# Decode attention keys turned in 32x32 blocks on VectorE instead of 128x128 on TensorE

## The chip, the core and the metric

The kernel runs on one core of a Trainium2 chip. The metric is the device time of one execution in microseconds; lower is better. In the profile PE is TensorE (matmuls), PEld its weight loads, DVE VectorE, ACT ScalarE, POOL GpSimd and SP the engine that issues most DMAs. SBUF has 128 partitions; a PSUM bank holds 128 partitions of 512 fp32 numbers.

## What is computed

One step of a two-layer decoder for a prompt of 512 tokens and a sample group of 8 sequences with 8 new tokens each, which have 2048 past tokens in a paged cache. Layer 0 is differential attention, layer 1 retention. The change touches only the sample group's attention over the cache:

```python
kp = cache_k[page_table].reshape(db, past, nh, 2, d)      # pages of 128 tokens, 8 heads, k1 | k2, d = 128
vp = cache_v[page_table].reshape(db, past, nh, -1)        # 256 wide
s_past = jnp.einsum('bqhcd,bkhcd->bchqk', q, kp)
s_new = jnp.einsum('bqhcd,bkhcd->bchqk', q, k_new)
sc = jnp.concatenate([s_past, s_new], axis=-1) * scale - slopes[:, None, None] * dist[None]
p = jax.nn.softmax(jnp.where(dist >= 0, sc, -jnp.inf), axis=-1)
p = p[:, 0] - lam * p[:, 1]
return einsum('bhqk,bkhe->bqhe', p[..., :past], vp) + einsum('bhqk,bkhe->bqhe', p[..., past:], v_new)
```

A score needs the 128 numbers of a head's key on the partitions, and a page arrives with its tokens on the partitions, so every page has to be turned. All is fp32.

## The kernel before

**Projections.** The bulk of the kernel is the projection matmuls (PE `project`, helper `mm`, L965). A weight chunk of 4x128x256 is split by ACT (WH, L1236) and DVE (WL, L1523) into a high and a low part, and each 128x128 weight tile meets the activations as WH·XH, WH·XL and WL·XH, each as two matmuls of 288 columns: six matmuls are one "projection tile". The program is written as one list of stages; `proj.tile()` is the beat, and everything else stands at a numbered slot before a tile (`attention_pair`, 256 slots for a pair of heads; `page_slot(k)` = 2 + 3.5 k). Every engine runs its own part of each stage in the list's order and waits on semaphores.

**The sample group's attention** is worked off in eight halves of 128 slots (a pair of heads, four of the eight sequences). In a half:

- `carry` (DVE, L1681), just ahead of the half, copies the new queries and keys (at the middle of a pair, "qk") or the new values and gates (at its end, "vg") out of the projection's results. `place_q` (DVE, L1599) at slot 0 spreads the queries into `qrow`, with zeros, so that the four sequences of a half fall on different rows.
- `load_k` (SP, L903) fetches a page of 128 tokens x 512 numbers (256 KB) into one of 4 ring places `Kr`. `page` turns it: 4 TensorE transposes of 128x128 (PE L1032, helper `tr`, L968) into bank 4 for even and bank 5 for odd pages; ACT copies the even ones to `KTs` (L1357, copy helper L1236), DVE the odd ones (L1605, the copy is L1610). Two pages stand at one slot, and such a pair comes every 3.5 slots: 64 pages in a half, 512 in all.
- A unit is four pages of one sequence. `qk` (PE L1040) multiplies it: four matmuls of 512 columns, each into its own 32 rows of bank 6 (two heads x two key halves). There are 16 units in a half, one every 7 slots. After four units (one from each sequence, added up in the bank) `row_scores` (DVE L1613) adds the bias and takes a maximum.
- `soft_new`, `soft_max`, `soft_exp`, `soft_norm` stand at slots 28, 118, 120 and 125. `soft_new` (PE L1050) is four matmuls of 64 columns into 32 rows each.
- In the next half `e_transpose` (slots 7, 11) turns the probabilities, and `value` (PE L1069) multiplies four pages of values by them, every 7 slots from slot 16 on, at the slot of a `qk`. `load_v` (SP L909) fetches four pages into a ring of 8 behind each `value`. Each value page has its own semaphore. `sample_sq` (slot 127 of every second half) needs DVE's `soft_norm` and mixing to be done.

SP is one queue: between slot A and slot A + 7 it issues four value loads, two key loads, two more key loads and most times one weight load (L890), in this order. A page's number is read from `pt` ahead of each cache load (L900).

Of the kernel before, what the change touches and what calls it, by code (L numbers as in the profile page):

```python
# [17 lines left out]
HEADS = 8  # L18
# [13 lines left out]
NPAIR = 1 + NGROUP + 1  # L32
# [3 lines left out]
def shape_tables():  # L36
# [7 lines left out]
    head, half, tok, own_b = r // 64, r // 32 % 2, r % 32 // BATCH, r % BATCH  # L44
    dist_past = PAST + tok[:, None] - np.arange(GROUP * PAGE)[None]
    out_head, out_tok = r % 32 // 16, r % NQ
    pick = (out_head[:, None] == np.arange(2)[None]).repeat(NQ, 1) * np.tile(out_tok[:, None] == np.arange(NQ)[None], (1, 2))
    rows = np.concatenate([dist_past, pick, (half == 0)[:, None], (half == 1)[:, None]], 1)
    row = np.arange(SMP)
    pairs = []  # L50
    for g in range(HEADS // 2):
        sl = slope[2 * g + head][:, None]
        ahead = sl * GROUP * PAGE * np.arange(NGROUP)[None]
        dn = tok[:, None] - (row % NQ)[None]
        new = [np.where((row[None] // NQ == (BATCH * q + own_b)[:, None]) & (dn >= 0), -sl * dn, MASKED) for q in range(2)]
        pairs.append(np.concatenate([-sl, ahead, 0 * sl] + new, 1))
# [34 lines left out]
def adds(s):  # L91
# [26 lines left out]
    if k == "store_x":  # L118
# [18 lines left out]
        "place_q": {"q_placed": 1},  # L137
# [31 lines left out]
    if k == "load_v":  # L169
        return {f"v_in{a['n'] % VRING}": 16}  # L170
    if k in ("page", "e_transpose"):
        n = 4 + a["n"] % 2
        return {f"full{n}": 1, f"drained{n}": 1}
# [77 lines left out]
class SampleAttention:  # L251

    def __init__(self):
        self.pages = [(a, q, kg, bl, kg * GROUP + pp) for a in range(HEADS // 2) for q in range(2) for kg in range(NGROUP)
                      for bl in range(BATCH) for pp in range(GROUP)]
# [4 lines left out]
    def load_k(self):  # L260
        n = self.k_loads
        if n >= len(self.pages):
            return []
        self.k_loads += 1
        a, q, _, bl, p = self.pages[n]
        return [Stage("load_k", n=n, pair=a, b=BATCH * q + bl, p=p, freed=self.page_of.get(n - KRING))]
# [9 lines left out]
    def keys(self, h):  # L276
# [5 lines left out]
        put(0, Stage("place_q", pair=h // 2, q=h % 2))  # L282
        units = NGROUP * BATCH
        for u in range(units):
            kg, bl = divmod(u, BATCH)
            for pp in range(GROUP):
# [3 lines left out]
                if pp == 0 and u:  # L290
                    put(slot(u * GROUP + pp), *self.scores(h, u - 1))
                put(slot(u * GROUP + pp), page, *self.load_k())
        put(page_slot(2 * units), *self.scores(h, units - 1))
# [6 lines left out]
    def scores(self, h, u):  # L300
        kg, bl = divmod(u, BATCH)
        n = (h * NGROUP * BATCH + u) * GROUP
        qk = Stage("qk", u=u, bl=bl, last_even=self.page_of[n + 2], last_odd=self.page_of[n + 3])
        self.qk_of[h * NGROUP * BATCH + u] = qk
        return [qk] + ([Stage("row_scores", kg=kg)] if bl == BATCH - 1 else [])
# [374 lines left out]
def hybrid_step_kernel(nc, x_prompt, x_sample, cache_k, cache_v, page_table, state_ret, norm_pre_attn, w_in_attn,  # L680
# [30 lines left out]
    with ctx:  # L711
# [34 lines left out]
        qT0, kT0, vT, vn0, kn = lay("qT0", [128, 2, T]), lay("kT0", [128, 2, T]), lay("vT", [128, 2, T]), lay("vn0", [128, 5, 256]), lay("kn", [128, 2, 256])  # L746
# [5 lines left out]
        sgS, vS = [lay(f"sgS{i}", [128, 4, SMP]) for i in range(2)], [lay(f"vS{i}", [128, 512]) for i in range(2)]  # L752
        sS, sN = lay("sS", [128, PAST]), lay("sN", [128, SMP])
        e_all, e_new = lay("e_all", [128, PAGES, 128]), lay("e_new", [SMP, 128])
        dist_past, picks = lay("dist_past", [128, GROUP * PAGE]), lay("picks", [128, 18])
        pair_row = lay("pair_row", [128, NPAIR + 2 * SMP])
        KTs = [lay(f"KTs{i}", [128, 4, GROUP * PAGE]) for i in range(2)]
        qrow = lay("qrow", [128, 4, 132])
        row_sign, oV = lay("row_sign", [128, 1]), lay("oV", [128, 512])
        gmax, ebias, lsum, row1 = lay("gmax", [128, 5]), lay("ebias", [128, 5]), lay("lsum", [128, 5]), lay("row1", [128, 2])  # L760
        oS, oQ = lay("oS", [128, 4, SMP]), lay("oQ", [128, 4, SMP])
        rsS = lay("rsS", [128, 128])
        sc, pT = lay("sc", [128, 2, 512]), lay("pT", [128, 512])
# [24 lines left out]
        used[0] = 6 * T  # L788
# [88 lines left out]
        def _(sp):  # L877
# [21 lines left out]
            def load_page(src, pair, b, p, to):  # L899
                page = sp.value_load(pt[0:1, b * PAGES + p:b * PAGES + p + 1], min_val=0, max_val=src.shape[0] - 1)  # L900
# [1065 lines left out]
```

## Time and profile before

| | us |
|---|---|
| median of 3 runs (3840.97 to 3844.4) | 3841.65 |
| span of the profiled execution, first to last instruction | 3828.5 |
| the difference, around the span | 13.15 |
| attention, first to last key load | 135 to 1635 |
| PE busy | 3709.1 (97%) |
| DVE busy | 1453.5 (38%) |
| ACT busy | 1123.9 (29%) |

PE's busy time is a union of matmuls that overlap; what an edit on PE is worth is read from the starts of the instructions in the timeline, not from durations. A matmul of fp32 with 32 weight columns appears as two records, a transpose as one, a projection matmul as one.

### The profile page before, as it was taken

To read this page: it belongs to the slowest core of one execution; us is meant where nothing else is said; L and a number is where in the kernel's file an instruction comes from. 1 tells how busy PE (TensorE), PEld (TensorE's weight loads), DVE (VectorE), ACT (ScalarE), POOL (GpSimd) and SP (SyncE) were. 2 spreads that over 40 slices of the span, in tenths; PEclk is the share of its full clock that TensorE was granted. 3 is DMA by queue.
4 is the path that set the end of the run, shared out by engine and by line. 5 is a ranking of instruction groups with operands and counts; after the bars stand their busy time and mean duration, and the time that the engine had idled before them with its cause. 6 is when DMAs were issued, how large, how long until landed. Compare 5 with 4: busy or idle time off the path is not lost.

```text
span 3828.5 us, 70107 instructions
## 1 busy us (share of the span) xinstructions
PE 3709.1 (97%) x26980; PEld 3275.7 (86%) x26980; DVE 1453.5 (38%) x2215; ACT 1123.9 (29%) x1808; POOL 150.6 (4%) x87
## 2 busy tenths in 40 slices
PE   7999999999999999989899999999999999999998
PEld 7987887888788877767898989999989899989998
DVE  4244334433443344323633333333333324243345
ACT  4233233323332333221422222222222222232223
POOL 1000000200020002002200000000000000000000
PEclk9999999999999999999999999999999999999999
DMA  5456778687768776764442525242424343443333
GB/s 172 151 177 188 239 239 237 212 244 236 238 210 245 238 237 215 244 197 168 135 139 83 165 83 166 79 164 85 160 86 161 94 149 98 163 138 130 108 122 121
DMA packets 472204, 642.91 MB, mean 168 GB/s; under 512 B 35649, under 2 KB 294850, under 8 KB 468738
## 3 DMA queue, kind: packets, MB, share of 16 engines
q1 hardware_dynamic: 407122, 565.92, 47.6%
q10 hardware_dynamic: 64336, 72.24, 5.6%
q8 instruction: 216, 3.54, 0.4%
q14 instruction: 114, 0.93, 0.1%
q0 software_dynamic: 416, 0.28, 0.1%
HBM read 566.09 MB, written 70.65 MB: 166 GB/s over the span
## 4 chain that ended last, share of the span: by engine, by line
PE 50%; DVE 2%; issue 1%; DMA 1%; ACT 1%; POOL 1%; SPq 1%; ACTq 0%; DVEq 0%; POOLq 0%
PE low_banks L965 42%; PE high_banks L965 6%; PE high_banks L968 1%; DMA area<-in_cache_v 1%; POOL area L1897 1%; DVE WL L1523 0%; ACT WH L1236 0%; DMA WR<-in_w_in_ret 0%; SPq L900 0%; SPq L901 0%; ACTq L1401 0%; DVE area L1782 0%; ACT area L1236 0%; DVE area L1545 0%; ACTq L1400 0%
## 5 line engine op out<-in xcount | busy, mean ns | idle before, releaser
L965 PE MATMUL low_banks<-XH,WH 128*128 128x288 f32 (+2 forms) x6656 | 1545.6, 310 | 42.0 <-DVE XL L1528 16.6
L965 PE MATMUL low_banks<-XH,WL 128*128 128x288 f32 (+2 forms) x6656 | 1455.4, 296 | 0.0
L965 PE MATMUL low_banks<-XL,WH 128*128 128x288 f32 (+2 forms) x6656 | 1452.6, 296 | 0.0
L965 PEld LDWEIGHTS low_banks<-XH,WH 128*128 128x128 f32 x6656 | 1080.4, 190 | 142.4 <-issue 96.0
L965 PEld LDWEIGHTS low_banks<-XH,WL 128*128 128x128 f32 x6656 | 1083.7, 189 | 0.0
L965 PEld LDWEIGHTS low_banks<-XL,WH 128*128 128x128 f32 x6656 | 1083.4, 189 | 0.0
L1523 DVE TENSOR_TENSOR WL<-WR,WH 128x1024 fp32r<-128x1024 f32 x436 | 533.4, 1223 | 817.8 <-ACT WH L1236 812.7
L1236 ACT ACTIVATE WH<-WR 128x1024 fp32r<-128x1024 f32 x436 | 461.2, 1058 | 923.4 <-PE low_banks L965 652.6
L965 PE MATMUL high_banks<-area 128*32 128x512 f32 (+8 forms) x3696 | 654.1, 547 | 16.1 <-DVE area L1554 5.6
L1236 ACT ACTIVATE area<-high_banks 128x512 f32<-128x512 f32 x480 | 270.2, 569 | 1139.4 <-PE high_banks L968 756.8
L968 PEld LDWEIGHTS high_banks<-eye_sb,area 128*128 128x128 f32 (+2 forms) x3080 | 352.4, 142 | 156.6 <-issue 116.8
L968 PE MATMUL high_banks<-eye_sb,area 128*128 128x128 f32 (+2 forms) x3080 | 439.1, 278 | 40.9 <-DVE area L1857 15.8
L965 PEld LDWEIGHTS high_banks<-area 128*32 128x32 f32 (+4 forms) x3696 | 239.6, 147 | 231.5 <-issue 205.0
L1610 DVE COPY area<-high_banks 128x512 f32<-128x512 f32 x256 | 177.0, 691 | 569.8 <-PE high_banks L968 477.7
L1897 POOL TENSOR_TENSOR area<-area,power 128x1 f32<-128x1 f32 (+4 forms) x67 | 126.6, 1890 | 3639.6 <-DVE area L1495 3168.9
L1299 ACT ACTIVATE area<-low_banks 128x288 f32<-128x288 f32 (+2 forms) x384 | 157.9, 411 | 346.8 <-PE low_banks L965 311.6
L1545 DVE TENSOR_TENSOR area<-low_banks,area 128x288 f32<-128x288 f32 (+2 forms) x160 | 73.2, 457 | 144.4 <-PE low_banks L965 134.7
L1782 DVE SCALAR_TENSOR_TENSOR area<-area,high_banks 128x512 f32<-128x512 f32 x128 | 87.2, 744 | 49.8 <-PE high_banks L965 49.8
L1763 DVE SCALAR_TENSOR_TENSOR area<-area,high_banks 128x512 f32<-128x512 f32 x48 | 35.8, 747 | 159.9 <-PE high_banks L965 157.9
L1795 DVE TENSOR_TENSOR area<-high_banks,area 128x512 f32<-128x512 f32 (+1 forms) x40 | 25.6, 640 | 113.5 <-PE high_banks L968 113.5
L1618 DVE SCALAR_TENSOR_TENSOR area<-area,high_banks 128x512 f32<-128x512 f32 x32 | 23.9, 747 | 66.6 <-PE high_banks L965 66.6
L1528 DVE TENSOR_TENSOR XL<-XL,XH 128x576 fp32r<-128x576 f32 (+1 forms) x48 | 36.1, 752 | 31.9 <-ACT XH L1236 30.7
(113 smaller groups left out, 840.9 us busy)
## 6 DMA issues: line engine op xcount, KB each, us to landing
area<-in_cache_k SPq DMA_DIRECT2D x512, 256.0 KB, 4.1
area<-in_cache_v SPq DMA_DIRECT2D x512, 256.0 KB, 4.1
WR<-in_w_in_ret SPq DMA_DIRECT2D x200, 512.0 KB, 3.5
WR<-in_w_in_attn SPq DMA_DIRECT2D x136, 512.0 KB, 5.4
out<-area ACTq DMA_DIRECT2D x73, 512.0 KB, 3.1
WR<-in_w_out_ret SPq DMA_DIRECT2D x68, 512.0 KB, 3.3
area<-in_state_ret SPq DMA_DIRECT2D x64, 512.0 KB, 5.6
WR<-in_w_out_attn SPq DMA_DIRECT2D x32, 512.0 KB, 5.5
```

Source lines behind the costliest of these rows:

```text
L965: return nc.tensor.matmul(out, a, b, start=start, stop=stop, skip_group_check=True)
L968: return nc.tensor.matmul(out, a, ident[0:n, 0:n], start=True, stop=True, is_transpose=True, skip_group_check=True)
L1236: return nc.scalar.activation(out, in_, ACT.Copy, scale=scale)
L1299: last = nc.scalar.activation(dst[:, lo:hi], bank[2 * cb + b][:, 0:hi - lo], f)
L1523: v.tensor_tensor(WL[:, slot, :, :], WR[:, slot, :, :], WH[:, slot, :, :].bitcast(f32), SUB).then_inc(sem["w_lo"], 1)
L1528: v.tensor_tensor(XL[:, kt, 0:width], XL[:, kt, 0:width].bitcast(f32), XH[:, kt, 0:width].bitcast(f32), SUB).then_inc(sem["w_lo"], 1)
L1545: last = v.tensor_tensor(dst[:, lo:hi], bank[2 * cb + b][:, 0:hi - lo], dst[:, lo:hi], ADD)
L1610: v.tensor_copy(KTs[u % 2][:, :, pp * 128:(pp + 1) * 128], bank[5][:, :].rearrange("p (j s) -> p j s", j=4)).then_inc(sem["drained5"], 1)
L1763: ins = v.scalar_tensor_tensor(out=Sp[:, e, :], in0=Sp[:, e, :], scalar=hc[:, 387:388], in1=bank[4 + e][:, :], op0=MUL, op1=ADD)
L1782: v.scalar_tensor_tensor(out=mine, in0=mine, scalar=hc[:, 388:389], in1=bank[4 + j][:, :], op0=MUL, op1=ADD).then_inc(sem[f"drained{4 + j} ...
L1795: v.tensor_tensor(to, o4, g4, MUL).then_inc(sem[f"drained{n}"], 1)
L1897: nc.gpsimd.tensor_tensor(out, a, power[0:R, 0:n], ALU.pow).then_inc(sem[name], 1)
```

## The change

Keys are turned by DVE in SBUF, in blocks of 32x32, and PE no longer touches the pages before `qk`. One DVE instruction takes two pages (128 x 2 x 16 x 32) into the new layout `KTs` [128, 16, 128]: block m holds the 32 numbers 32 m .. 32 m + 31 of the keys, on partition 32 a + i stands number i of token quarter a. The stages stay at their slots; `page` does nothing for the first page of a pair, and both key loads stand behind the second. The order of units changes: all four units of one sequence come one after the other, so `row_scores` is by sequence.

`qk` becomes 16 matmuls of 128 columns for a unit (four blocks of the head's 128 numbers, added up, for each of four 32-row outputs) with queries that are zero except in the rows of their token quarter. `place_q` makes these queries with 16 PE matmuls against slices of the identity and four DVE copies. PE's first act in a half is now to wait for `carried`. Softmax statistics are shared among the four quarters of a token by small DVE transposes (`stat`, `row_all`). Value pages are loaded so that their tokens follow the new order: 32 partitions at a stride of 4, four places each; the four pages of a group raise one semaphore.

```diff
         "place_q": {"q_placed": 1},
+        "place_q": {"full4": 1, "drained4": 1},
...
-                put(slot(u * GROUP + pp), page, *self.load_k())
+                put(slot(u * GROUP + pp), page, *([*self.load_k(), *self.load_k()] if pp % 2 else []))
...
             def load_k(g, n, pair, b, p, freed):
                 if freed is not None:
-                    bank_sem = f"full{4 + freed.a['n'] % 2}"
-                    sp.wait_ge(sem[bank_sem], c.after(freed, bank_sem))
+                    sp.wait_ge(sem["k_turned"], c.after(freed, "k_turned"))
...
+                sp.dma_start(Vr[t:128:GROUP, half * GROUP:(half + 1) * GROUP, :],
+                             cv[page, :, pair * 512:(pair + 1) * 512].rearrange("a (o j) n -> j (a o) n", o=4)
+                             ).then_inc(sem[f"v_in{half}"], 16)
...
-            def page(g, n, u, pp, freed):                       # PE
-                ...
-                for j in range(4):
-                    last = tr(bank[b][:, j * 128:(j + 1) * 128], Kr[:, slot, j * 128:(j + 1) * 128])
+            def place_q(g, pair, q):                            # PE
+                pe.wait_ge(sem["carried"], c.before("carried"))
+                free(4)
+                ...
+                for d in range(4):
+                    for a in range(4):
+                        last = mm(spread[32 * a:32 * a + 32, d], ident[:, 32 * d:32 * d + 32], mine)
+                last.then_inc(sem["full4"], 1)
...
+            def qk(g, u, bl, kg, placed, turned):
+                pe.wait_ge(sem["k_turned"], c.after(turned, "k_turned"))
+                pe.wait_ge(sem["drained4"], c.after(placed, "drained4"))
                 pe.wait_ge(sem["s_drained"], c.before("s_drained"))
-                for j in range(4):
-                    last = mm(bank[6][32 * j:32 * j + 32, :], qrow[:, j, 32 * bl:32 * bl + 32], KTs[u % 2][:, j, :],
-                              start=bl == 0, stop=bl == BATCH - 1)
+                for d in range(4):
+                    for j in range(4):
+                        last = mm(bank[6][32 * j:32 * j + 32, kg * 128:(kg + 1) * 128], qrow[:, bl * 16 + 4 * j + d, :],
+                                  KTs[u % 2][:, 4 * j + d, :], start=d == 0, stop=d == 3)
...
             def page(g, n, u, pp, freed):                       # DVE
+                if pp % 2 == 0:
+                    return
+                slot = n % KRING - 1
+                for k in (slot, slot + 1):
+                    dve.wait_ge(sem[f"k_in{k}"], START[f"k_in{k}"] + 16 * (n // KRING + 1))
+                if freed is not None:
+                    dve.wait_ge(sem["qk_done"], c.after(freed, "qk_done"))
+                v.transpose(KTs[u % 2][:, :, 32 * pp - 32:32 * pp + 32].rearrange("p m (t i) -> p t m i", t=2),
+                            Kr[:, slot:slot + 2, :].rearrange("p t (m i) -> p t m i", i=32)).then_inc(sem["k_turned"], 1)
```

On DVE `row_scores` becomes four additions of 128 columns and a maximum in place of one addition of 512 and a maximum; `soft_max` goes from 3 to 5 instructions; `soft_norm` from 5 (the last over 2048 columns) to 12 (the last four over 512 each). ACT loses its copies of the even pages.

On PE, at a unit with values in the second half (before): the value matmuls, `qk` (32x512) and the transposes of two pages stand between two projection tiles.

```order
L965 MATMUL high_banks<-area 32x512 [waits pv_drained,v_in0,drained5,drained4]
L965 MATMUL high_banks<-area 32x512 [waits v_in1]
L965 MATMUL high_banks<-area 32x512 [waits v_in2]
L965 MATMUL high_banks<-area 32x512 [waits v_in3]
L965 MATMUL high_banks<-area 32x512 [waits q_placed,s_drained,drained5,drained4]
L965 MATMUL high_banks<-area 32x512 x3
L968 MATMUL high_banks<-eye_sb,area 128x128 [waits drained4,k_in0]
L968 MATMUL high_banks<-eye_sb,area 128x128 x3
L968 MATMUL high_banks<-eye_sb,area 128x128 [waits drained5,k_in1]
L968 MATMUL high_banks<-eye_sb,area 128x128 x3
L965 MATMUL low_banks<-XH,WH 128x288 [waits w_lo]
```

The same place on PE now:

```order
L975 MATMUL high_banks<-area 32x512 [waits pv_drained,v_in0,drained5,drained4]
L975 MATMUL high_banks<-area 32x512 x3
L975 MATMUL high_banks<-area 32x128 [waits s_drained,drained4,k_turned]
L975 MATMUL high_banks<-area 32x128 x15
L975 MATMUL low_banks<-XH,WH 128x288 [waits w_lo]
```

The transposes and PE's waits for key loads are gone, and `qk` waits for DVE's `k_turned`.

On PE, at the start of a half (before); the projection goes on at once:

```order
L965 MATMUL low_banks<-XH,WH 128x288 [waits proj0_drained,x_lo,w_lo]
L965 MATMUL low_banks<-XH,WH 128x288
L965 MATMUL low_banks<-XL,WH 128x288 x2
L965 MATMUL low_banks<-XH,WL 128x288 x2
```

The same place on PE now; `32x16x8` are the matmuls of `place_q`:

```order
L975 MATMUL low_banks<-XL,WH 128x288 x2
L975 MATMUL low_banks<-XH,WL 128x288 x2
L975 MATMUL high_banks<-area,eye_sb 32x16x8 [waits drained4,carried]
L975 MATMUL high_banks<-area,eye_sb 32x16x8 x15
L975 MATMUL low_banks<-XH,WH 128x288 [waits proj0_drained,x_lo,w_lo]
L975 MATMUL low_banks<-XH,WH 128x288
```

All projection tiles of the half now stand behind a wait for `carried`.

On DVE, in a half with prompt work (before): a copy of an odd page, then the parts of the output and of a weight chunk.

```order
L1610 COPY area<-high_banks 128x4x128 [waits qk_done,full5]
L1592 SCALAR_TENSOR_TENSOR area<-high_banks,subln,area 128x128 [waits proj1_drained,gated_out,proj0_drained,full4]
L1592 SCALAR_TENSOR_TENSOR area<-high_banks,subln,area 128x128 [waits dve_order]
L1610 COPY area<-high_banks 128x4x128 [waits qk_done,full5]
L1523 TENSOR_TENSOR WL<-WR,WH 128x1024 [waits w_hi]
```

The same place on DVE now:

```order
L1623 STREAM_TRANSPOSE area<-area 128x2x16x32 [waits qk_done,k_in1,k_in0]
L1597 SCALAR_TENSOR_TENSOR area<-high_banks,subln,area 128x128 [waits proj1_drained,gated_out,proj0_drained,full4]
L1597 SCALAR_TENSOR_TENSOR area<-high_banks,subln,area 128x128 [waits dve_order]
L1623 STREAM_TRANSPOSE area<-area 128x2x16x32 [waits qk_done,k_in3,k_in2]
L1528 TENSOR_TENSOR WL<-WR,WH 128x1024 [waits w_hi]
```

The wait for the key loads (`k_in`) has moved from PE to DVE, ahead of the work queued there.

## Rows read from the trace of the kernel before

**Rows 1.** The page, part 1: busy us, share of the span, instructions.

```profile
PE 3709.1 (97%) x26980; PEld 3275.7 (86%) x26980; DVE 1453.5 (38%) x2215; ACT 1123.9 (29%) x1808; POOL 150.6 (4%) x87
```

**Rows 2.** Windows over seven runs of 14 blocks: window, length, busy, clock, DMA, GB/s.

```profile
527.50:680.60 153.10, 151.16 (x1147) 122.02 (x1146) 57.50 (x106) 49.06 (x87) 2.56 (x3) 1.00 0.82 246
...
sum 1069.90, PE 1051.74 PEld 846.07 DVE 403.69 ACT 324.88 POOL 16.45; mean PE 150.25 PEld 120.87 DVE 57.67 ACT 46.41 POOL 2.35
```

**Rows 3.** Timeline of PE over one unit: start, length, instruction, count, idle before.

```profile
207.47 0.43 PE L965 MATMUL low_banks<-XH,WL 128*128 128x288 f32 x2
207.83 1.06 PE L965 MATMUL high_banks<-area 128*32 128x512 f32 x8
208.83 1.09 PE L968 MATMUL high_banks<-eye_sb,area 128*128 128x128 f32 x8
209.68 0.51 PE L965 MATMUL low_banks<-XH,WH 128*128 128x288 f32 x2
...
212.15 1.03 PE L968 MATMUL high_banks<-eye_sb,area 128*128 128x128 f32 x8
212.94 0.52 PE L965 MATMUL low_banks<-XH,WH 128*128 128x288 f32 x2
213.29 0.43 PE L965 MATMUL low_banks<-XL,WH 128*128 128x288 f32 x2
```

**Rows 4.** Timeline of PE at `soft_new`: short matmuls of 32 weight columns.

```profile
178.36 0.32 PE L965 MATMUL high_banks<-area 128*32 128x64 f32 x8
178.61 0.53 PE L965 MATMUL low_banks<-XH,WH 128*128 128x288 f32 x2
178.98 0.29 PE L965 MATMUL low_banks<-XL,WH 128*128 128x288 f32 x1
```

**Rows 5.** Lines by form: busy, mean ns of one, idle before and releaser.

```profile
L1523 DVE TENSOR_TENSOR WL<-WR,WH 128x1024 fp32r<-128x1024 f32 x436 | 533.4, 1223 | 817.8 <-ACT WH L1236 812.7 <-issue 3.8
L965 PE MATMUL high_banks<-area 128*32 128x512 f32 x2304 | 306.8, 608 | 5.1 <-DMA area<-in_cache_v 3.2 <-DVE area L1652 1.7
L1610 DVE COPY area<-high_banks 128x512 f32<-128x512 f32 x256 | 177.0, 691 | 569.8 <-PE high_banks L968 477.7 <-issue 89.7 <-DVE WL L1523 1.1
L1775 DVE TENSOR_SCALAR area<-area 128x512 f32<-128x512 f32 x40 | 18.0, 485 | 5.6 <-POOL area L1897 5.3
L965 PE MATMUL high_banks<-area 128*32 128x64 f32 x64 | 2.6, 231 | 0.0
```

**Rows 6.** Timeline of DVE and then PE around the middle of a pair ("qk").

```profile
502.38 1.29 DVE L1642 TENSOR_SCALAR area<-area 128x2048 f32<-128x2048 f32 x1
...
508.67 0.23 DVE L1694 COPY area<-area 128x128 f32<-128x128 f32 x1
...
506.18 0.43 PE L965 MATMUL low_banks<-XH,WH 128*128 128x288 f32 x2
```

**Rows 7.** Timeline of DVE and then PE around the end of a pair ("vg").

```profile
699.81 0.29 DVE L1687 COPY area<-area 128x256 f32<-128x256 f32 x1
...
697.67 0.42 PE L965 MATMUL low_banks<-XH,WH 128*128 128x288 f32 x2
```

**Rows 8.** Timeline of SP's DMA issues over one block (start, from first to last issue).

```profile
548.94 3.64 SPq L901 DMA_DIRECT2D area<-in_cache_v  x4
553.38 3.66 SPq L901 DMA_DIRECT2D area<-in_cache_k  x4
557.09 0.96 SPq L890 DMA_DIRECT2D WR<-in_w_in_attn  x1
```

**Rows 9.** The key loads by tile: issue ns min/median/max; us to landing min/median/max.

```profile
L901 SPq DMA_DIRECT2D area<-in_cache_k x512: 332/333/976, 135.3 to 1634.8; - x171
...
DMA to landing us min/median/max: 2.9/4.1/8.5
```

**Rows 10.** Waits of SP's queue from 330 to 1640: total us, times, longest.

```profile
SPq L900 <- PE high_banks L965: 141.9, 85, 4.5
SPq L900 <- PE high_banks L968: 87.3, 65, 11.9
```

More of the change, by code:

```diff
@@ L52, in shape_tables @@
         sl = slope[2 * g + head][:, None]
-        ahead = sl * GROUP * PAGE * np.arange(NGROUP)[None]
         dn = tok[:, None] - (row % NQ)[None]
-        new = [np.where((row[None] // NQ == (BATCH * q + own_b)[:, None]) & (dn >= 0), -sl * dn, MASKED) for q in range(2)]
-        pairs.append(np.concatenate([-sl, ahead, 0 * sl] + new, 1))
+        new = [np.where((row[None] // NQ == (BATCH * q + quarter)[:, None]) & (dn >= 0), -sl * dn, MASKED) for q in range(2)]
+        pairs.append(np.concatenate([-sl] + new, 1))
     bias_pairs = np.stack(pairs)
@@ L169, in adds @@
     if k == "load_v":
[L170 to L171 removed]
+        return {f"v_in{a['n'] // GROUP % 2}": 16}
+    if k == "page":
+        return {"k_turned": 1} if a["pp"] % 2 else {}
+    if k == "e_transpose":
         n = 4 + a["n"] % 2
@@ L281, in keys @@
         slot = lambda n: page_slot(n // 2)
-        put(0, Stage("place_q", pair=h // 2, q=h % 2))
+        placed = Stage("place_q", pair=h // 2, q=h % 2)
+        put(0, placed)
         units = NGROUP * BATCH
         for u in range(units):
-            kg, bl = divmod(u, BATCH)
             for pp in range(GROUP):
@@ new lines, in row_scores @@
+            def row_scores(g, bl):
+                cols = slice(bl * 512, (bl + 1) * 512)
+                for n in ("qk_done", "full4", "full5", "bias_sample_in"):
+                    dve.wait_ge(sem[n], c.before(n))
+                in_turn = lambda a: a.rearrange("p (j t) -> p j t", t=GROUP)
+                for kg in range(NGROUP):
+                    part = slice(kg * 128, kg * 128 + 128)
+                    ins = v.scalar_tensor_tensor(out=in_turn(sS[:, bl * 512 + kg * 128:bl * 512 + kg * 128 + 128]), in0=in_turn(dist_past[:, part]),
+                                                 scalar=pair_row[:, 0:1], in1=bank[6][:, part].rearrange("p (t j) -> p j t", t=GROUP),
+                                                 op0=MUL, op1=ADD)
+                    if kg < NGROUP - 1:
+                        o.link(ins)
+                    else:
+                        ins.then_inc(sem["s_drained"], 1)
@@ new lines, in soft_norm @@
+                o.link(v.transpose(stat_T[:], stat[:]))
+                o.link(v.reduce_sum(stat_8[:], by_token, AX.X))
+                o.link(v.reciprocal(stat_8[:], stat_8[:]))
+                rows_back()
+                o.link(v.tensor_scalar(row_all[:, 0:BATCH], row_all[:, 0:BATCH], row_sign[:], None, MUL))
+                o.link(own_row(row_new[:]))
+                o.link(v.tensor_scalar(sN[:], sN[:], row_new[:], None, MUL))
+                for n in range(BATCH):
+                    part = sS[:, n * 512:(n + 1) * 512]
+                    ins = v.tensor_scalar(part, part, row_all[:, n:n + 1], None, MUL)
+                    if n < BATCH - 1:
+                        o.link(ins)
+                    else:
+                        ins.then_inc(sem["e_normed"], 1)
```

157 lines of the change are left out of this document (74 added, 83 removed).

## The prediction, made before the changed kernel had been run

> **What bounds the kernel now.** The page's first part says PE: 97% busy, DVE 38%, ACT 29% [rows 1]. That average hides stages, so I read the windows over the seven runs of 14 blocks in which keys and values are both loaded (a block is 7 slots, from one `qk` to the next): PE is busy 1051.7 of 1069.9 us, DVE 404, at full clock [rows 2]. A block lasts 1069.9 / 98 = 10.92 us on average. So an instruction taken from PE there is time won, unless the next limit comes first. The next limit is not DVE but SP's queue. In the SP timeline four cache loads take 3.64 us from the first to the last issue, of which the last issue is 0.33, so one load occupies the queue for (3.64 - 0.33) / 3 = 1.10 us [rows 8, 9]. A block needs eight of them, 8.8 us, and most times a weight load, 0.4 to 1.0 [rows 8]: 9.5 us. In the wait view SP was held by PE for 141.9 + 87.3 = 229 us between 330 and 1640 [rows 10]: that is its reserve, and the change eats into it.
>
> **Edit 1: pages off PE, `qk` in short matmuls.** From the PE timeline over one unit without values [rows 3]. Before: `qk` starts 0.36 us after the last projection step's start where a step takes 0.26 (entry 0.10); `qk` and the first two pages take from 207.83 to 209.68 (1.85); the second two pages 0.79 (212.15 to 212.94), and the step after them 0.35 where 0.26 is usual (0.09), which holds after the first two pages as well. Sum 0.10 + 1.85 + 0.09 + 0.88 = 2.92 us a unit.
> After: 16 matmuls of 128 columns, four side by side in four groups of 32 weight columns, each two records: eight rounds. How long is a round? At 512 columns two rounds take 1.06 - 0.61 = 0.45 for the distance of one [rows 3, 5]. At 64 columns the distance is 0.32 - 0.23 = 0.09 [rows 4, 5]. The line through both gives 0.14 for 128; without any fixed part, 0.45 / 4 = 0.11. I take 0.125, since in a series the next weights can load under the running round. Entry 0.10 as above; exit by `soft_new`: 0.25 to the next projection step less two rounds of 0.09, and 0.37 for that step instead of 0.26, together 0.18 [rows 4]. Sum 0.28 + 8 x 0.125 = 1.28 us. A unit saves 1.64 (1.52 to 1.78). There are 8 x 16 = 128: **-210 us** (-195 to -228). 512 ACT and DVE copies go too, from engines with room: nothing.
>
> The trace's short matmuls give 0.02 to 0.03 us of fixed part in a round. The Trainium skill, page "TensorEngine Tiling (Array Packing)", section "Performance Considerations", has each matmul carry some 60 cycles. An estimate from that page, if all 32 records of a unit paid it in turn, is 0.8 us a unit, and the gain would shrink by about 100 us.
>
> **Edit 2: `place_q` on PE, behind `carried`.** 16 matmuls of 128 columns like `qk`: 8 x 1.28 = **+10 us**. Before them PE waits for DVE's `carry`, and all projection tiles of the half are queued behind that wait. At a "qk" boundary PE began slot 128 at 506.18 and `carry` ended at 508.67 + 0.23 = 508.90: 2.7 us [rows 6]. At a "vg" boundary 697.67 and 700.10: 2.4 [rows 7]. Four of each: **+20 us**. It can't be hidden: `carry` needs the last tile's evacuation, which PE has only just fed. Then DVE makes four copies of 512 columns from PSUM, 4 x 0.69 [rows 5], before bank 4 is free; PE's prompt `scores` at slot 2 want it. And `soft_norm` ends in four instructions of 512 columns (0.485 each, [rows 5]) instead of one of 1.29 [rows 6], plus seven small ones: about 1.7 us later for `sample_sq` at slot 127, four times. Against that, short waits of PE that were there shrink. Together **+6 us** (0 to 20).
>
> **Edit 3: DVE turns.** 256 instructions of 2 x 512 numbers. No row shows one. Nearest: the weight split, 1024 numbers a partition from SBUF to SBUF, 1.22 us [rows 5]; I take that. A floor is one copy of 512, 0.69; a ceiling twice 1.22, should a turn pass numbers at half that rate. At 1.22 DVE gains 2 x (1.22 - 0.69) = 1.1 us a block on 404 / 98 = 4.1 [rows 2, 5], 5.2 in 9.3: it has room. But it now waits for the keys, ahead of its weight splits and the prompt's softmax. After slot A the queue issues four values, then two keys; the second is issued at about A + 1 + 4.4 + 1.9 = 7.3 us and lands 4.1 later [rows 9], at A + 11.4, while DVE's place in the program comes at A + 9.3. So DVE stands some 2 us in every block. PE asks for the block's turned keys only 3.5 slots later and for a weight split 6 tiles later; I put **+8 us** (0 to 30) for the prompt's chain.
>
> **The queue.** A block on PE becomes 10.92 - 1.64 = 9.28 us, SP needs 9.5. On average that is 0.22 x 98 = 22 us, if SP could run ahead without limit. It can't: key places are four, so long blocks give nothing back. Against that stands a lag of about 3 us that PE tolerates in each of the seven runs. I take 3 us a run: **+21 us** (0 if the lag absorbs it, 45 if a value load in the new form [32, 4] takes 0.1 us longer to issue, which is 0.4 x 98 = 39 more less the tolerance). In the tail, where PE only waits for values, all four loads must be in: **+2 us**.
>
> **Sum.** -210 + 10 + 20 + 6 + 8 + 21 + 2 = -143. The sum is made on the profiled execution: 3828.5 - 143 = 3685.5, with the 13.15 around the span 3698.6 against the median. I say 3698.
>
> **Rivals.**
> - *Neither queue nor keys hold anyone.* SP has 229 us of waits in reserve [rows 10]. Then -210 + 38 = -172: 3670. Against it: 9.28 is below 9.5.
> - *DVE becomes the bound.* At 2.45 us a turn, DVE has 4.1 - 1.4 + 4.9 = 7.6 us of work and 2 of waiting in a block, 9.6, in order, and stalls of PE on top: some 0.5 us x 98 = 49 on top, 3747. For it: no row shows a turn. The Trainium skill, page "VectorE: DVE Perf Modes", section "The three transpose paths", gives 311 ns for a 128x128 turn on VectorE in bf16. An estimate from that page, eight times as much for two pages, is 2.5 us; the trace's rows have no turn to set beside it.
> - *Short rounds cost 0.20 us*, because four weight loads a round don't hide under 128 columns: 8 x 0.075 x 136 = +82, 3780. `soft_new`'s 0.09 at 64 columns speaks against it [rows 4, 5].
> - *Slower than before: the value loads.* Each now writes four places on 32 partitions at a stride. If such a load holds SP longer by x, a block is 9.5 + 4x. Outside the 98 blocks the change gains 30 x 1.64 - 38 = 11 us, 0.11 a block, so it decides from 9.5 + 4x = 11.03, x = 0.38 us, i.e. 1.48 a load instead of 1.10. At x = 0.5: 98 x (11.5 - 11.03) = +46, 3888. Issues of 0.33 have few outliers (up to 0.98, [rows 9]).
>
> **How the numbers follow.** Forecast 3698 (its own range 3665 to 3730): 0.58. First rival 0.15, DVE 0.12, rounds 0.08, value loads 0.05; 0.02 for about no change. The range must hold 0.8: 3650 (rounds of 0.11 and a free queue: -228 + 38 = -190) to 3760 (the DVE rival and part of the queue's bound); the last three cases lie outside. A measurement of this kernel can tell 0.2% from no change. Faster by more than that 0.92, within it 0.02, slower 0.06.
>
> **What would show it.** PE records of 128 columns on 32 weight columns, 2048 matmuls for `qk`, a unit of 1.28 us between projection steps, no transposes of pages. A DVE turn of about 1.2 us, 256 times, with waits on key loads. At each half's start a PE wait of 2 to 3 us on DVE's `carry`. SP waits far below 229 us and blocks with values at 9.4 to 9.6. It would be wrong if those blocks reached 10 us, if a turn took over 2 us, or if the value loads landed later than 4 us.

## The result, and the profile after

The changed kernel takes 3853.6 us (median of 11 runs, 3842.8 to 3863.5), the kernel before 3837.8 (11 runs, 3827.8 to 3844.4). The ratio is 1.0039, 95% interval 1.0028 to 1.0049: slower by 0.4%. The forecast was 3698, the range 3650 to 3760, and it gave "slower" 0.06.

The page of the changed kernel, part 1, against [rows 1]:

```profile
span 3851.8 us, 71863 instructions
PE 3566.1 (93%) x28260; PEld 3196.8 (83%) x28260; DVE 1647.2 (43%) x2424; ACT 983.2 (26%) x1552; POOL 150.7 (4%) x87
```

PE's busy time fell by more than 140 us and the span rose by 23.3. That compares two single executions; by the medians the change costs 15.8. (The 13.15 us that I had called "around the span" are mostly this scatter: the timed executions on record are only 1.8 to 2.8 us longer than their spans, so the profiled one of before was a quick one. The forecast, 143 us under the median, does not depend on it.) What was won as work came back as waiting. Where, the wait view from 130 to 1640 tells (us in total, times, longest):

```profile
DVE area L1623 <- DMA area<-in_cache_k: 521.3, 185, 12.4
...
PEld high_banks L975 <- DVE area L1623: 98.7, 49, 8.4
...
PE high_banks L975 <- DVE area L1623: 63.0, 34, 8.2
```

PE and its weight loads wait for turned keys (L1623), and DVE, which turns them, stands 521 us for the key loads. The loads themselves, by line (issue in ns, min/median/max; us from issue to landing), first the keys, to be set beside [rows 9], then the values:

```profile
L913 SPq DMA_DIRECT2D area<-in_cache_k x512: 327/333/1162, 132.8 to 1633.4; - x171
...
DMA to landing us min/median/max: 2.9/4.3/8.7
```

```profile
L920 SPq DMA_DIRECT2D area<-in_cache_v x512: 602/602/1192, 266.4 to 1770.3; - x171
...
DMA to landing us min/median/max: 3.6/4.3/7.4
```

Both land as fast as keys did before, to 0.2 us. But a value load in its new shape holds SP 0.60 us instead of 0.33. The SP timeline over one block, answering [rows 8] (start, from first to last issue, instruction, count):

```profile
549.16 4.92 SPq L920 DMA_DIRECT2D area<-in_cache_v  x4
554.87 3.68 SPq L913 DMA_DIRECT2D area<-in_cache_k  x4
558.59 0.43 SPq L897 DMA_DIRECT2D WR<-in_w_in_attn  x1
559.80 4.74 SPq L920 DMA_DIRECT2D area<-in_cache_v  x4
```

From one value group to the next 10.64 us pass, and what lies between the issues is register work: with 4.75 for four value issues one load takes (4.75 - 0.60) / 3 = 1.38 us, before 1.10. In the wait view of SP from 514 to 650 there are 4.3 us of waits in 136; SP's long waits (175.8 us for L1623 between 130 and 1640) lie elsewhere: 72 us before 320, where only keys are loaded, and most of the rest at the half boundaries. Inside the halves with values **the queue sets the pace**. A block of 10.6 us is also past the 10 at which the prediction called itself wrong.

### The profile page after: what moved, and what is told of

It is laid out like the page before. It is cut to its first block, busy times and chain, and to the rows that moved or that the text cites. A ratio compares the mean times of both kernels' runs of the same rounds, so it can differ in the third digit from the quotient of the medians.

```text
span 3851.8 us, 71863 instructions
## 1 busy us (share of the span) xinstructions
PE 3566.1 (93%) x28260; PEld 3196.8 (83%) x28260; DVE 1647.2 (43%) x2424; ACT 983.2 (26%) x1552; POOL 150.7 (4%) x87
## 4 chain that ended last, share of the span: by engine, by line
PE 50%; DVE 1%; issue 1%; SPq 1%; ACT 1%; POOL 1%; DMA 1%; ACTq 0%; DVEq 0%; POOLq 0%
PE low_banks L975 43%; PE high_banks L975 6%; PE high_banks L978 1%; POOL area L1939 1%; DMA area<-in_cache_v 1%; SPq L920 0%; DVE WL L1528 0%; SPq L907 0%; ACT WH L1248 0%; ACTq L1405 0%; DVE area L1824 0%; ACT area L1248 0%; ACT XH L1248 0%; DVE area L1550 0%; DMA WR<-in_w_in_ret 0%
## 5 line engine op out<-in xcount | busy, mean ns | idle before, releaser
L975 PEld LDWEIGHTS low_banks<-XH,WH 128*128 128x128 f32 x6656 | 1097.5, 192 | 189.5 <-issue 125.6
L975 PE MATMUL high_banks<-area 128*32 128x128 f32 (+6 forms) x6768 | 677.8, 392 | 127.4 <-DVE area L1623 63.0
L975 PEld LDWEIGHTS high_banks<-area 128*32 128x32 f32 (+2 forms) x6768 | 331.4, 135 | 351.8 <-issue 218.5
L1623 DVE STREAM_TRANSPOSE area<-area 128x1024 f32<-128x1024 f32 x256 | 318.7, 1245 | 548.1 <-DMA area<-in_cache_k 521.3
L1248 ACT ACTIVATE area<-high_banks 128x512 f32<-128x512 f32 (+1 forms) x224 | 119.1, 537 | 646.0 <-PE high_banks L978 341.9
L978 PE MATMUL high_banks<-eye_sb,area 128*128 128x128 f32 (+2 forms) x1032 | 160.8, 278 | 51.3 <-DVE area L1899 16.0
L978 PEld LDWEIGHTS high_banks<-eye_sb,area 128*128 128x128 f32 (+2 forms) x1032 | 124.1, 142 | 57.1 <-issue 47.4
L1824 DVE SCALAR_TENSOR_TENSOR area<-area,high_banks 128x512 f32<-128x512 f32 x128 | 87.2, 745 | 50.1 <-PE high_banks L975 50.1
L1805 DVE SCALAR_TENSOR_TENSOR area<-area,high_banks 128x512 f32<-128x512 f32 x48 | 35.8, 747 | 159.8 <-PE high_banks L975 157.9
L1322 ACT ACTIVATE area<-area 128x128 f32<-128x128 f32 (+3 forms) x64 | 36.0, 563 | 115.8 <-DVE area L1563 100.1
L1633 DVE SCALAR_TENSOR_TENSOR area<-area,high_banks 128x128 f32<-128x128 f32 x128 | 44.5, 347 | 23.9 <-PE high_banks L975 14.6
```

The source lines that it names most:

```text
L975: return nc.tensor.matmul(out, a, b, start=start, stop=stop, skip_group_check=True)
L978: return nc.tensor.matmul(out, a, ident[0:n, 0:n], start=True, stop=True, is_transpose=True, skip_group_check=True)
L1248: return nc.scalar.activation(out, in_, ACT.Copy, scale=scale)
L1322: ins = nc.scalar.activation(sc[:, cc, 0:n], sc[:, cc, 0:n], ACT.Exp, bias=pst[:, cc:cc + 1], accum_out=pst[:, 2 + cc:3 + cc])
L1623: v.transpose(KTs[u % 2][:, :, 32 * pp - 32:32 * pp + 32].rearrange("p m (t i) -> p t m i", t=2), Kr[:, slot:slot + 2, :].rearrange("p t ( ...
L1633: ins = v.scalar_tensor_tensor(out=in_turn(sS[:, bl * 512 + kg * 128:bl * 512 + kg * 128 + 128]), in0=in_turn(dist_past[:, part]), scalar= ...
```

## One stretch in nine kernels

From the second unit of the second half to its last value group lie 15 unit intervals, the same work in each kernel. I read its length with the windows view. Columns: window, length, then busy time of PE, PEld, DVE, ACT, POOL (instructions), granted clock, DMA share, GB/s. Before, then changed:

```profile
527.46:688.30 160.84, 158.90 (x1205) 128.14 (x1205) 61.46 (x115) 50.88 (x92) 3.11 (x4) 1.00 0.81 243
```

```profile
513.00:672.20 159.20, 142.67 (x1341) 118.84 (x1340) 78.43 (x130) 34.02 (x60) 3.10 (x4) 0.95 0.83 245
```

PE has 16 us less to do and the stretch is 1.6 us shorter. The experiments below fill this table (the lengths are read in the same way from one profiled run each; medians of whole runs beside them; e1's profiled run is 15 us under its median, e2's 9 over):

| kernel | stretch, us | per unit | clock | whole, us |
|---|---|---|---|---|
| before | 160.8 | 10.72 | 1.00 | 3838 |
| before, strided values (e2) | 169.0 | 11.27 | 1.00 | 3895 |
| before, no bounds test (e9) | 160.6 | 10.71 | 1.00 | 3820 |
| before, fixed pages (e10) | 160.3 | 10.69 | 1.00 | 3807 |
| changed | 159.2 | 10.61 | 0.95 | 3854 |
| changed, plain values (e1) | 148.9 | 9.93 | 0.97 | 3762 |
| changed, no bounds test (e5) | 143.5 | 9.57 | 1.00 | 3712 |
| changed, fixed pages (e6) | 137.0 | 9.13 | 1.00 | 3657 |
| changed, fixed pages, plain values (e11) | 136.9 | 9.13 | 1.00 | 3657 |

## Experiments: the queue and the order of loads

Theory Q says that SP's work per block sets the pace. Its rivals: B, pauses of PE at the boundaries; K, keys issued behind values; S, the strided shape as such.

**e1, changed kernel with plain value loads.**

```diff
-                sp.dma_start(Vr[t:128:GROUP, half * GROUP:(half + 1) * GROUP, :],
-                             cv[...].rearrange("a (o j) n -> j (a o) n", o=4)
+                sp.dma_start(Vr[:, half * GROUP + t, :],
+                             cv[...].rearrange("a s n -> s (a n)")
```

> The changed kernel with only its value loads back in the old shape: 128 partitions of one place, 2 KB each, as before. (The values then lie in other rows than the weights expect, so the sample outputs are not the reference's; work, bytes and waits are the same.) Theory Q, the queue: in the changed kernel four value loads take 4.75 us on SP from the first to the last issue, (4.75 - 0.60) / 3 = 1.38 each, where before it was 1.10; a block of SP is 4 x 1.38 + 4 x 1.12 + 0.8 = 10.8 us and sets the pace. With the old shape it is 9.7, so 98 blocks give back 1.1 us each and the tail's 16 value groups as much: 3853 - 108 - 18 = 3727, between 3715 and 3760. Theory B, pauses: PE's waits for late turns, for place_q and for the half boundaries set the pace and the queue only fills the time they leave; then only the tail gains: 3835, and not under 3810.

Measured 3761.7 us (3746.5 to 3766.8), 0.9809 of before (0.9788 to 0.9831). The issue is back to 332/333 ns. Some 90 us came back from 0.27 us a load: Q's figure (108 + 18) was high, with the result 2 us outside its range, and B's far off.

**e2, kernel before with the changed kernel's value loads,** the reverse edit with the group's semaphore.

> The kernel before with only the changed kernel's value loads (32 partitions at a stride, four places, one semaphore for four pages); pages still go over PE. (The values lie in other rows than the weights expect, so the sample outputs are not the reference's.) Theory Q: SP's block becomes 4 x 1.38 + 4 x 1.10 + 0.8 = 10.7 us against 10.92 of PE: just under, so the 14-block runs lose 0 to 0.3 us a block, and the tail, which waits for values, loses 1.1 us x 16 = 18: 3838 + 18 + 0 to 30 = 3856 to 3886. Theory B: the loads' shape matters only in the tail: 3845 to 3858.

3895.4 us, ratio 1.0151 (1.0128 to 1.0173): 58 us slower, beyond both figures. PEld now stands 96.9 us for key loads between 130 and 1640, where keys go straight to PE. I had priced 0.1 us of margin between queue (10.7) and PE (10.92) on averages; units differ in length (7.7 to 16.2 us in the table's stretch before), and a queue without margin loses in the short ones and gets nothing back in the long ones, since key places are four. The edit also makes PE wait for four pages at once, and how much of the 58 that is I did not part from the rest.

**e3, keys issued before values in a slot:** `sorted(x, key=lambda s: s.kind == "load_v")` over each slot's stages.

> The changed kernel with one thing moved: in a slot that issues four value loads and two key loads, the key loads are issued first. Nothing is left out. Theory K, the keys: DVE stood 521 us for key loads, because they are issued behind 4 x 1.38 = 5.5 us of value loads; with keys first they land 5.5 us earlier in each block, DVE's wait for them falls by more than 200 us, PE's 162 us of waits for the turns fall by half or more: 3853 - 60 = about 3790, between 3760 and 3820. Theory Q: SP's work per block stays 10.8 us, so the pace stays: 3840 to 3860.

3870.1 us, ratio 1.0092 (1.0069 to 1.0116): 16 us slower than the changed kernel. DVE's wait for keys only fell from 521 to 467 us and PE's for the turns rose. Theory K falls. My reading is that in a queue that is full all the time, being ahead of four loads shifts the phase, not the pace. That is not the whole of it: 3870 is also 10 us above Q's range, and why it became slower no run shows.

**e4, value loads issued from ACT's queue.**

> The changed kernel with its value loads, in their new shape, issued from ACT's queue instead of SP's. Nothing is left out. Theory Q: SP's block falls to 4 x 1.12 + 0.8 = 5.3 us and no longer sets a pace; ACT has room (26% busy) for 4 x 0.6 and the register loads, about 5.5 us a block at the most. If the queue was the limit: 3853 - 110 (pace) - 10 (tail) = 3735 or less, down to 3690. Theory B: no more than 20 us gained: 3833 or more. A risk in both: ACT then waits for PE's values in its own order, and its splits and evacuations stand behind that wait; then it could be slower than 3853.

3924.2 us, ratio 1.0223 (1.02 to 1.0246). This misses Q's number by 190 us, and by the risk named. The queue was relieved: DVE's wait for keys is down to 164 us. But ACT, in order, stands at `pv_done` with the weight splits behind it. The waits between 130 and 1640, of DVE and then of SP:

```profile
DVE WL L1531 <- ACT WH L1240: 238.0, 59, 10.9
...
SPq L897 <- DVE WL L1531: 392.9, 73, 15.5
```

The first was 29.7 us in the changed kernel. So e4 neither confirms nor refutes Q; e5 and e6 relieve the queue without burdening another engine.

**e8, values two and two instead of four at once.**

```diff
-            for c in range(GROUP):
-                put(t, *self.load_v())
+            put(t, *self.load_v(), *self.load_v())
+            put(page_slot(2 * m + 5), *self.load_v(), *self.load_v())
```

> The changed kernel with its four value loads of a unit issued as two at the unit's first half and two at its second, each ahead of two key loads, instead of four at once. Nothing is left out. SP's work is the same, but the longest stretch in which keys stand behind values is halved, 5.5 to 2.8 us. Theory Q: the same pace, 3843 to 3863. Theory K2, the burst: DVE's waits come from the burst of four; its key wait falls by 150 us or more and the time by 30 or more: under 3823.

3849.8 us (3843.9 to 3858.2), ratio 1.0038 (1.0026 to 1.0051): no different from the changed kernel, as Q says; DVE's wait for keys stays at 507 us, and K2 falls.

**e5, no bounds test of the page number.**

```diff
-                return bass.ds(sp.value_load(pt[...], min_val=0, max_val=src.shape[0] - 1), 1)
+                return bass.ds(sp.value_load(pt[...]), 1)
```

> The changed kernel, cache loads without the bounds test of the page number. Nothing is left out of what is computed. In SP's records of the changed kernel a load has, beside the 0.33 or 0.60 us of the issue, 0.27 of table read, then some 0.25 of the bounds test (register operation 0.15, assertion 0.02 and the gaps), then 0.15 of address. Without it a block of SP is 10.8 - 8 x 0.25 = 8.8 us, under PE's 9.3. Theory Q (the queue set the pace; the plain value shape alone gave 92 us for 1.1 us a block): at least as much, 3853 - 92 to 130 = 3723 to 3761. Theory S, the shape: the strided loads harm by how they land and not by how long SP is held; then 3835 to 3853.

3711.6 us (3709.0 to 3722.8), ratio **0.9684** (0.9667 to 0.97): some 140 us faster than the changed kernel and 3.2% under the kernel before, by an edit that touches nothing but SP's register instructions. It went below my 3723 to 3761. SP's timeline, at the same place in the program:

```profile
511.47 3.89 SPq L920 DMA_DIRECT2D area<-in_cache_v  x4
...
526.67 3.12 SPq L913 DMA_DIRECT2D area<-in_cache_k  x4
```

(3.89 - 0.60) / 3 = 1.10 us a value load and (3.12 - 0.33) / 3 = 0.93 a key load: 4 x 1.10 + 4 x 0.93 + 0.8 = 8.9 us a block, under PE's 9.13. Yet the pace is 9.57 and the whole is 54 us above e6: a mean below the engine's own is not enough to free it.

**e9, the same edit in the kernel before.**

> The kernel before, its cache loads without the bounds test. Nothing is left out. Its SP waited 265 us for other engines between 330 and 1640, so in the runs of blocks PE sets the pace and a faster queue gives little; the tail, in which PE waits for values, gains 16 x 4 x 0.25 = 16 us. Theory Q: 3837 - 10 to 22 = 3815 to 3827. If the queue already held the kernel before, in stretches, as much as it held the changed one: under 3800, and then the changed kernel's gain from the same edit (142 us) is no sign that the change itself met the queue.

3820.2 us, ratio 0.996 (0.9945 to 0.9975). Some 15 us, where the changed kernel gained 140. The table's stretch did not move (10.72 to 10.71); what moved is the tail, from its first value group to its last 85.0 us instead of 90.2, and some 7 us ahead of it that I did not place. So before, the queue did not hold the blocks; the change made it do so.

**e6, page numbers written into the program.**

```diff
-                return bass.ds(sp.value_load(pt[...], min_val=0, max_val=src.shape[0] - 1), 1)
+                return slice(b * PAGES + p, b * PAGES + p + 1)
```

> The changed kernel with page numbers written into the program instead of read from the page table (other pages than the reference's are read, as many and as large; the sample outputs are therefore not the reference's). Both shapes of load stay. SP's block falls to about 4 x 0.65 + 4 x 0.38 + 0.8 = 5 us: the queue is out of the question as a limit. Theory Q alone: DVE's wait for keys falls from 521 us to under 100, PE follows its own 9.3 us: 3700 or less. Theory C, stalls and clock: PE's stalls at the half boundaries and the half-clock stretches behind them stay (the granted clock over 155 to 1640 stays at 0.95 to 0.97), and the time stops at 3715 to 3745.

3657.4 us (3654.4 to 3661.0), ratio 0.953. Theory Q's figure, 41 us below my forecast and still inside its range (3650 to 3760). A forecast with the queue left out would have been near: the first rival said 3670. The stretch:

```profile
483.60:620.60 137.00, 134.86 (x1341) 114.51 (x1340) 77.72 (x130) 34.13 (x60) 3.10 (x4) 1.00 0.89 287
```

The same PE instructions as in the changed kernel's stretch, 22.2 us faster, PE busy 98% of it. Of the 22.2 us, 7.8 are busy time (142.67 against 134.86 for the same 1341 records, at clock 0.95 against 1.00), 14.4 waiting. DVE's key waits did not fall under 100 but to 208 us in all; with PE following its own pace they cost little. Theory C's 3715 to 3745 is missed too, although the clock over 155 to 1620 stayed at 0.97.

**e10, fixed pages in the kernel before.**

> The kernel before with page numbers written into the program (other pages are read, as many and as large; sample outputs are not the reference's). The tail gains 16 x 4 x 0.7 = up to 45 us until values' landing or PE holds it; the runs of blocks little. 3790 to 3820. Set beside the changed kernel with fixed pages (3657), it gives what the change is worth when the queue holds neither: my prediction's sum without the queue was -172; Theory Q says -135 to -172. If it comes under 3760, the change's work on PE is worth less than 105 us and the prediction's first term is wrong as well.

3807.2 us (3805.2 to 3814.5), ratio 0.9932. The difference to e6 is what the change is worth when no queue holds either: by the ratios (0.9530 - 0.9932) x 3838 = **-154 us**. With the intervals of the two ratios that is good to some 9 us, and it lies in Q's range.

**e11, fixed pages and plain values.**

> The changed kernel with fixed page numbers and its value loads in the plain shape (128 partitions, one place). The sample outputs are not the reference's. With fixed pages SP has only 5 us of work in a block. Theory H: the strided shape costs only by holding SP (0.60 against 0.33 us an issue); with the queue idle half the time it costs nothing, 3657 as with the strided shape (3647 to 3662). Theory S: it costs by slower landing or by crossing other transfers: then 20 us or more are won here too, under 3637.

3657.3 us (3657.0 to 3659.4) against e6's 3657.4. With a queue that has time, the strided shape costs nothing: what it cost in e1's comparison is 0.27 us of SP a load, and not its landing or its rows. Theory S falls.

## Experiments: the boundaries

**e7, `place_q` at slot 4 instead of slot 0:** `put(4, placed)`.

> The changed kernel with place_q moved from slot 0 of a half to slot 4; the first qk is at slot 9. Nothing is left out. Theory C: at slot 0 PE waits 2.6 to 3.9 us for carry and falls to half clock after it; at slot 4 carry is long done, so 8 x (2.7 + 2) = 38 us are won, less about 1 us for each e_transpose at slot 7 that waits for bank 4: 3853 - 30 = 3823, between 3810 and 3840. Theory Q: what PE wins there it loses again to the queue within the half; 3845 to 3855.

3836.1 us (3829.2 to 3852.2, 10 runs), ratio 1.0002 (0.9988 to 1.0015): some 15 us better than the changed kernel, about half of what theory C had but within its range, and more than Q allowed. So not everything that PE wins at a boundary is lost to the queue again.

**e12, `place_q` at slot 4 and no bounds test.**

> The changed kernel without the bounds test and with place_q at slot 4 instead of 0. Nothing is left out. Without the bounds test it took 3712; place_q at slot 4 gave 17 us while the queue still set the pace. Theory C: with the queue relieved, time won at a half's start is no longer lost again within the half: 3712 - 17 to 38 = 3674 to 3695. If boundary and queue are one and the same loss, counted twice: 3705 to 3712.

3706.3 us (3693.9 to 3719.7), ratio 0.9671 (0.9645 to 0.9697), beside e5's 0.9684 (0.9667 to 0.97). The intervals overlap: 5 us at the most likely, and inconclusive. Theory C's 3674 to 3695 is missed. The waits show why little comes of it: in e7 PE's waits at `place_q` for `carry` are gone from the view and a new one stands there, `e_transpose` and the prompt waiting for bank 4 behind DVE's four copies:

```profile
PE high_banks L978 <- DVE area L1609: 15.2, 8, 2.3
```

## Why the prediction was wrong, step by step

**"Queue +21", the step that failed.** The medians of before differ by 4 us from one group of runs to the next, so I take ratios times 3838; each difference below is good to some 8 us. The queue costs the changed kernel (1.0039 - 0.9530) x 3838 = 195 us (e6), and cost the kernel before (1 - 0.9932) x 3838 = 26 (e10). The change added 169 where the sum had 21, and 2 in the tail. -154 + 169 = +15, the whole result. The 169 have two parts (88 and 79; e6 and e11, equal in time, differ by 2 us in ratio).
- *The value load's issue*, (1.0039 - 0.9809) x 3838 = 88 us (e1). I took 0.33 for a shape that no row showed, and bounded it at 0.1 us more (for a term of up to 45 us, where 22 + 39 less 7 x 3 gives 40). The row gives 0.27 more. The bound had no ground in a row; a weight load, also of more than two dimensions and of twice the bytes, stood in [rows 8] with 0.4 to 1.0 and was the nearest one.
- *The rest*, (0.9809 - 0.9535) x 3838 = 105 (e1 to e11), less the 26 of before: 79. I set SP's 9.5 us against PE's 9.28 and got 0.22 a block. With plain values the pace was 9.93 (e1), without the queue 9.13 (e11): 0.80 a unit, over some 100 units 80 us. SP's end was right: in e1's stretch its wait view has 6.5 us, so it worked (148.9 - 6.5) / 15 = 9.49 us a block. PE's end was 0.15 too high. The other 0.44 a block are the failure proper: SP itself stood still in that time although the pace was above the work of both, and I had taken for granted that a lag of 3 us a run covers it. e5 shows it too, with SP's work below PE's. That four key places are too few for units of such uneven length is the likely reason; no run changes their number. The small difference of two averages carried the whole term.

The rival "slower value loads" had the mechanism and the place, decided from x = 0.38 and measured 0.27: the kernel came out slower nevertheless, because the plain queue already took 79 us that this rival's threshold did not count. It had a chance of 0.05. Of the reserve of 229 us that I read in [rows 10], 128 lie in the seven runs of blocks (the wait view of SP over each), 1.3 us a block; the rest lies at the boundaries, where it is no help to a block. The new shape alone takes 4 x 0.27 = 1.1 of the 1.3, and PE's block became 1.6 shorter.

**"Edit 1, -210": right.** One `qk` of the changed kernel, PE timeline, against [rows 3]:

```profile
209.70 0.43 PE L975 MATMUL low_banks<-XH,WL 128*128 128x288 f32 x2
210.06 1.09 PE L975 MATMUL high_banks<-area 128*32 128x128 f32 x32
211.08 0.54 PE L975 MATMUL low_banks<-XH,WH 128*128 128x288 f32 x2
211.46 0.43 PE L975 MATMUL low_banks<-XL,WH 128*128 128x288 f32 x2
```

Entry 0.10, eight rounds 1.02 (0.1275 each, taken as 0.125), exit 0.12: 1.24 us against 1.28 predicted, so 1.68 saved. The same unit in e10 and in e6, each from its value group to the next:

```profile
521.08 1.96 PE L965 MATMUL high_banks<-area 128*32 128x512 f32 x16
530.44 1.95 PE L965 MATMUL high_banks<-area 128*32 128x512 f32 x16
```

```profile
483.64 1.98 PE L975 MATMUL high_banks<-area 128*32 128x512 f32 x40
491.34 1.98 PE L975 MATMUL high_banks<-area 128*32 128x512 f32 x40
```

9.36 becomes 7.70, 1.66 less. The rival of 0.20 us a round falls, and so does the estimate from the Trainium skill, page "TensorEngine Tiling (Array Packing)", section "Performance Considerations": by it the 32 records of a unit would have carried some 0.8 us on top of their columns, and all 32 took 1.02 together, where I had 1.00.

**"Edit 2, +36": under-sized.** With fixed pages the whole is -154, and 128 units at 1.66 make -212, so 58 us are lost elsewhere, where I had 36 here. Most of it lies at the boundaries. e6 and e10, around the end of a pair; the last value group, then the waits until the first `qk`:

```profile
620.65 2.10 PE L975 MATMUL high_banks<-area 128*32 128x512 f32 x10
...
630.73 0.70 PE L975 MATMUL high_banks<-area,eye_sb 128*128 128x256 f32 x2 [1.90 <-DVE area L1704]
...
635.10 2.07 PE L975 MATMUL high_banks<-area,eye_sb 128*32 128x128 f32 x32 [2.30 <-DVE area L1729]
...
641.80 1.19 PE L975 MATMUL high_banks<-area 128*128 128x128 f32 x4 [2.35 <-DVE area L1609]
...
650.35 1.09 PE L975 MATMUL high_banks<-area 128*32 128x128 f32 x32
```

```profile
681.39 2.10 PE L965 MATMUL high_banks<-area 128*32 128x512 f32 x10
...
693.85 1.06 PE L968 MATMUL high_banks<-eye_sb,area 128*128 128x128 f32 x8 [0.89 <-DVE area L1554]
...
702.15 1.07 PE L965 MATMUL high_banks<-area 128*32 128x512 f32 x8
```

29.7 us against 20.8. At the middle of a pair the loss is smaller, 23.3 us (452.41 to 475.67) against 20.2 (491.21 to 511.43). The waits of PE in e6 from 130 to 1640 name the parts:

```profile
PE high_banks L975 <- DVE area L1729: 11.4, 4, 4.5
PE high_banks L975 <- DVE area L1704: 10.7, 4, 6.1
PE high_banks L975 <- DVE area L1736: 10.5, 4, 2.7
PE high_banks L975 <- DVE area L1609: 10.1, 4, 2.8
```

The wait for `carry` (L1729, L1736) was sized right: 21.9 us against 20. Wrong were `place_q` itself, 2.07 us behind that stall instead of 1.28, and the +6 for the rest: DVE's `sample_sq` (L1704) holds PE 10.7 us where e10 has 4.4, and the four copies, 4 x 1.07 us instead of 4 x 0.69, hold the prompt's `scores` at bank 4 for 10.1 (2.35 here). Waits and `place_q` (8 x 2.07) come to 59 us, less those 4.4 to 55, about what is missing. I had also left out that the next key loads stand behind those copies, since DVE frees the key places only after them.

**The clock, a term I did not have.** After some stalls of about 2 us TensorE runs at the lower of its two levels. Changed kernel, DVE, then PE, then two windows:

```profile
592.24 1.25 DVE L1623 STREAM_TRANSPOSE area<-area 128x1024 f32<-128x1024 f32 x1 [5.04 <-DMA area<-in_cache_k]
593.41 0.70 DVE L1597 SCALAR_TENSOR_TENSOR area<-high_banks,subln,area 128x128 f32<-128x128 f32 x2
```

```profile
594.25 0.41 PE L978 MATMUL high_banks<-eye_sb,area 128*128 128x128 f32 x2 [2.20 <-DVE area L1597]
...
595.53 0.68 PE L975 MATMUL low_banks<-XH,WH 128*128 128x288 f32 x2
596.01 0.68 PE L975 MATMUL low_banks<-XL,WH 128*128 128x288 f32 x2
```

```profile
594.00:598.00 4.00, 3.75 (x19) 3.78 (x20) 2.48 (x3) 0.87 (x2) 0.00 (x0) 0.62 0.81 237
602.00:606.00 4.00, 4.00 (x57) 3.23 (x55) 2.63 (x5) 1.06 (x1) 0.55 (x1) 1.00 0.92 302
```

This is the whole chain of loss in small. A key load is late, DVE stands 5.04 us for it, the prompt's drain L1597 stands behind it in DVE's order, PE waits 2.20 us for that drain, and then its steps are 0.48 us apart (1.2 GHz) instead of 0.26 (2.4 GHz). From 155 to 1620 the granted clock is 0.95, before it was 1.00, 0.97 in e5 and e6. In the table's stretch the longer busy time was 7.8 of the 22.2 us between the changed kernel and e6. How much of it is a loss of its own is not parted by any run: where the queue sets the pace, a faster PE might only have waited longer.

**"Edit 3, +8": the turn right, its cover wrong.** 1.245 us a turn (1.22 taken); the DVE rival falls, and with it the 2.5 us estimated from the Trainium skill, page "VectorE: DVE Perf Modes", section "The three transpose paths". DVE's waits were 521 us, more than twice my 2 us a block, since the queue ran late; with the queue relieved PE waited 2.8 us for turns (e6).

**"Tail +2": under-sized.** From the first value group of the tail to its last, 1659.73 to 1749.9 before and 1660.0 to 1774.2 after: 24 us. The queue carries little but values there, and each of 64 costs it 0.27 more, 17 us; PE's waits for values between 1655 and 1770 went from 3.2 to 21.4, and the clock from 0.98 to 0.79. As it happens the two profiled executions reach 1660 together: up to there the change had won and lost the same, and the tail made it slower. (By the medians, which lie 15.8 us apart and not 23.3, it may have been some 7 us ahead there.)

## What to carry to other kernels

When work moves off the bounding engine, price the next limit to a tenth of a microsecond, and first: an issuing queue has a cost per load made of register work and of the load's shape; at the same 256 KB the shape alone moved the issue from 0.33 to 0.60 us. A difference of two nearly equal paces is no term to put a point value on; its range is that of both paces times the number of units, and even a queue a little faster than the engine can cost some tenths of a microsecond a unit (e5: 9.57 where neither needs more than 9.13). And look for the cheap remedy in the queue itself: dropping a bounds test turned a loss of 0.4% into a gain of 3.2% (e5), the best kernel here that computes the same outputs, together with e12, which the measurement can't tell from it.

## What the runs showed of the hardware

- A load of 256 KB held SP's queue 0.33 us as 128 rows of 2 KB, and 0.60 us as 32 partitions at a stride with four rows of 2 KB each; both landed after 4.3 us in the changed kernel. A weight load of 512 KB held it 0.43. With a queue that has time the second costs nothing (e6 and e11, 3657 both).
- Of the 1.10 us of a load with a page number from a table, only 0.33 are the issue; without the bounds test it takes 0.93 (e5).
- DVE turned 1024 fp32 numbers a partition in 32x32 blocks in 1.245 us, as long as a subtraction of the same size, SBUF to SBUF (1.216). Four copies of 512 columns from PSUM on 32 partitions each, written at a stride, took 1.07 us apiece against 0.69 for one on 128 partitions written in runs of 128 numbers.
- Sixteen fp32 matmuls of 128 columns, four side by side, took 1.02 us in a row.
- With the queue relieved, DMA engines are 0.89 busy at 287 GB/s in the stretch (e6), where it was 0.81 at 243 before, and keys land after 5.7 us instead of 4.1. Whether that is the next limit no run tests.
